# Two-layer hybrid encoder, one core: projections that fill TensorE's waits move from 64x64 tiles to the whole array in part, and items, weights and merges are reordered

## The reference, cut to what matters

```
x += 1/2 * g0 * norm(swiglu(mod0(norm(x))))
x +=       g1 * norm(mixer(mod1(norm(x))))      # h = mod1(norm(x))
x += 1/2 * g2 * norm(swiglu(mod2(norm(x))))

proj = h @ w_in                                  # columns for r, m, d and the gates
y_r = rwkv7(...)      # 16 heads x 64, delta rule in both directions
y_m = mamba2(...)     # z (2048 columns), xbc (3072, depthwise conv over 5 tokens, then silu), dt
y_d = diff_attention  # q, k, v (3072 columns), 8 heads, two softmax maps per head
merged = g[0]*(y_r @ w_br_r) + g[1]*(y_m @ w_br_m) + g[2]*(y_d @ w_br_d)
mixer = merged @ w_out
```

## Time and profile before

| | |
|---|---|
| median of 3 runs | 2737.28 us (2736.98 to 2739.47) |
| the profiled execution's own time | 2737.22 us |
| its span, first to last instruction | 2735.5 us |
| instructions of the program | 66483 |
| busy: PE / DVE / ACT / POOL | 2620.0 / 1413.6 / 499.4 / 232.0 us |
| mean granted TensorE clock | 0.993 of 2.4 GHz |
| moved by DMA | 445.12 MB |

### The profile page before, as it was taken

The page is one execution under the profiler, slowest core; times in us unless marked ns, Lnnn a source line. Parts: engine busy times, 40 slices in busy tenths (PEclk is TensorE's granted clock), DMA queues, the critical chain, the costliest instruction groups (busy, mean ns, idle before and its releaser), DMA issues.

```text
span 2735.5 us, 66483 instructions
## 1 busy us (share of the span) xinstructions
PE 2620.0 (96%) x30077; PEld 1906.3 (70%) x30077; DVE 1413.6 (52%) x2560; ACT 499.4 (18%) x1016; POOL 232.0 (8%) x372
## 2 busy tenths in 40 slices
PE   6999999999999999999999999999999899999999
PEld 6777877777775555577787778777778745546776
DVE  3552465677775856312035425456787768562001
ACT  1000223122222332100010011322222223221000
POOL 6000102000001101100000010110000011100000
PEclk9999999999999999999999999999999999999999
DMA  9894433322327542484469734423222275424452
GB/s 364 309 337 151 133 117 123 111 83 92 116 80 239 169 168 94 144 291 165 157 242 340 271 128 142 152 91 113 87 83 88 91 253 191 143 96 154 138 168 93
DMA packets 226348, 445.12 MB, mean 163 GB/s; under 512 B 7545, under 2 KB 102327, under 8 KB 226065
## 3 DMA queue, kind: packets, MB, share of 16 engines
q1 hardware_dynamic: 211376, 395.59, 41.5%
q0 software_dynamic: 12960, 38.98, 4.5%
q10 hardware_dynamic: 1728, 6.29, 0.6%
HBM read 422.88 MB, written 17.96 MB: 161 GB/s over the span
## 4 chain that ended last, share of the span: by engine, by line
PE 81%; DVE 11%; ACT 3%; issue 2%; DMA 2%; POOL 1%; DVEq 0%; ACTq 0%; SPq 0%; POOLq 0%
PE ps L1039 79%; DVE scratch L2228 5%; DVE scratch L2231 2%; DVE scratch L2234 1%; DVE gbc L2234 1%; PE ps L1068 1%; DVE scratch L2544 1%; DMA scratch<-in_ada_w 1%; DMA ring<-in_w_in 1%; DMA scratch<-acs_scratch 0%; DMA acs_scratch<-scratch 0%; ACT scratch L2053 0%; ACT scratch L2051 0%; ACT scratch L2200 0%; DVE x L2234 0%
## 5 line engine op out<-in xcount | busy, mean ns | idle before, releaser
L1039 PE MATMUL ps<-hT,ring 64*64 64x256 f32 (+3 forms) x9472 | 1147.9, 367 | 8.3 <-issue 3.1
L1039 PEld LDWEIGHTS ps<-hT,ring 64*64 64x64 f32 (+2 forms) x9472 | 943.0, 160 | 155.9 <-issue 35.8
L1039 PE MATMUL ps<-scratch 64*64 64x32 f32 (+6 forms) x15264 | 846.7, 255 | 56.8 <-DVE scratch L2228 16.1
L1039 PEld LDWEIGHTS ps<-scratch 64*64 64x64 f32 (+2 forms) x15264 | 592.6, 140 | 332.3 <-issue 206.2
L2228 DVE TENSOR_TENSOR scratch<-scratch,ps 128x256 f32<-128x256 f32 (+3 forms) x314 | 155.2, 494 | 661.1 <-ACT scratch L1895 533.1
L1039 PE MATMUL ps<-ring,hT 64*64 64x256 f32 (+2 forms) x2816 | 425.4, 421 | 5.3 <-DVE scratch L2234 2.6
L1039 PEld LDWEIGHTS ps<-ring,hT 64*64 64x64 f32 (+1 forms) x2816 | 228.7, 149 | 143.3 <-issue 116.8
L2228 DVE TENSOR_TENSOR scratch<-scratch 128x512 f32<-128x512 f32 (+4 forms) x426 | 276.1, 648 | 75.4 <-ACTq L2035 31.8
L1039 PE MATMUL ps<-ring,scratch 128*128 128x512 f32 x512 | 234.7, 593 | 0.5
L2234 DVE SCALAR_TENSOR_TENSOR scratch<-scratch,ccol 128x1024 f32<-128x1024 f32 x120 | 154.2, 1285 | 15.2 <-DMA scratch<-in_ada_w 11.3
L1895 ACT ACTIVATE scratch<-ps 128x512 f32<-128x512 f32 x40 | 23.9, 597 | 746.1 <-PE ps L1039 746.1
(11 more groups left out here) (228 smaller groups left out, 1392.8 us busy)
## 6 DMA issues: line engine op xcount, KB each, us to landing
ring<-in_w_in SPq DMA_DIRECT2D x56, 2048.0 KB, 9.0
ring<-in_ffn_w SPq DMA_DIRECT2D x88, 1024.0 KB, 9.0
scratch<-in_ada_w SPq DMA_DIRECT2D x35, 2048.0 KB, 16.2
scratch<-in_ffn_w SPq DMA_DIRECT2D x44, 1024.0 KB, 5.0
ring<-in_w_branch_mamba SPq DMA_DIRECT2D x8, 2048.0 KB, 8.0
scratch<-acs_scratch POOLq DMA_DIRECT2D x24, 512.0 KB, 5.8
scratch<-fill_scratch SPq DMA_DIRECT2D x16, 512.0 KB, 8.7
ring<-in_w_branch_rwkv SPq DMA_DIRECT2D x4, 2048.0 KB, 11.1
```

Source lines behind the costliest of these rows:

```text
L1039: return pe.matmul(o, lhsT, rhs, start=start, stop=stop)
```

## The change

- `FILL` gets a new order (c 0 comes before z 3, and so on). The steps are distributed anew over pairs and places, still 448 from pair 0 on; the levels lose steps in pairs 1 to 3 (3 to 2 in each), the place `s2` gains (4 to 6 in most pairs), and `fill(p, "k4")` is new, in the last level.
- `fill_mixed` replaces `fill_tiles`: steps at the places `TILE_POINTS` (`r0` to `u3`) are on tiles, a multiple of four of them in an item, and all others on the whole array. By the table, 112 of the 448 steps of a layer are on tiles and 336 on the whole array. Six items of 14 have no tile step and so no wait between turns.
- ACT's `conv_sigmoid` is put ahead of the item copies at `k4` and `u0`. The first convolution moves from pair 2 to pair 1, with three taps in a level.
- POOL computes `group_norm_rstd` before `next_pair`, and stores z 3 one pair later.
- The FFN's second weights are issued on ACT's queue instead of SP's.
- In attention, `beside` gets one more product before the last transposes of a head; the merges of the Mamba branch are cut in halves and put into heads 2, 3, 5 and 6; the attention branch's products are reordered so that 21 of 32 can come before the last rows of the last head, and its merges are reordered. The first output weights are loaded in two parts, the first earlier.
- At the start of layer 0, ACT instead of DVE copies the parameters (line 2343).

```diff
-FILL = [("z", 0), ("z", 1), ("z", 2), ("z", 3), ("c", 0), ("q", 0), ("c", 1), ("q", 1), ("c", 2), ("q", 2),
-        ("c", 3), ("q", 3), ("c", 4), ("c", 5), ("v", 0), ("v", 1)]
+FILL = [("z", 0), ("z", 1), ("z", 2), ("c", 0), ("z", 3), ("c", 1), ("q", 0), ("c", 2), ("q", 1), ("c", 3),
+        ("q", 2), ("c", 4), ("q", 3), ("c", 5), ("v", 0), ("v", 1)]
 # columns: ops mid lv k0 k1 k2 k3 (k4) r0 u0 s1 r1 u1 s2 r2 u2 s3 r3 u3 end
-FILL_PAIR = ((8, 8, 8, 2, 2, 2, 2, 0, 2, 0, 1, 1, 4, 1, 2, 0, 2, 2, 3),
-             (14, 10, 10, 3, 3, 3, 3, 0, 2, 0, 1, 1, 4, 1, 2, 0, 2, 2, 3),
-             (14, 10, 10, 3, 3, 3, 3, 0, 2, 0, 1, 1, 4, 1, 2, 0, 2, 2, 3),
-             (14, 10, 10, 3, 3, 3, 3, 0, 2, 0, 1, 1, 4, 1, 2, 0, 2, 2, 3),
-             (14, 8, 7, 1, 2, 2, 2, 0, 1, 0, 1, 1, 3, 1, 1, 0, 1, 1, 3),
-             (11, 8, 8, 2, 2, 2, 2, 0, 2, 0, 1, 2, 4, 2, 2, 0, 2, 2, 9),
-             (8, 8, 8, 2, 2, 2, 2, 0, 2, 0, 1, 1, 4, 1, 2, 0, 2, 2, 3),
-             (14, 8, 7, 1, 2, 2, 2, 0, 1, 0, 1, 1, 3, 1, 1, 0, 1, 1, 0))
+FILL_PAIR = ((7, 8, 8, 2, 2, 2, 2, 1, 0, 1, 0, 1, 1, 4, 1, 1, 0, 1, 1, 2),
+             (12, 7, 7, 2, 2, 2, 2, 1, 0, 2, 0, 1, 1, 6, 1, 2, 0, 1, 2, 2),
+             (13, 8, 7, 2, 2, 2, 2, 1, 0, 2, 0, 1, 2, 6, 1, 2, 0, 2, 2, 2),
+             (13, 8, 7, 2, 2, 2, 2, 1, 0, 2, 0, 1, 1, 6, 1, 2, 0, 2, 2, 2),
+             (13, 9, 9, 2, 3, 3, 3, 3, 0, 2, 0, 1, 1, 6, 1, 2, 0, 2, 2, 2),
+             (13, 8, 9, 3, 3, 3, 3, 3, 0, 1, 0, 1, 1, 4, 1, 1, 0, 1, 1, 2),
+             (12, 7, 7, 2, 2, 2, 2, 1, 0, 2, 0, 1, 1, 6, 1, 2, 0, 1, 2, 2),
+             (13, 8, 7, 2, 2, 2, 2, 1, 0, 2, 0, 1, 1, 6, 1, 2, 0, 2, 2, 8))
+TILE_POINTS = ("r0", "u0", "s1", "r1", "u1", "s2", "r2", "u2", "s3", "r3", "u3")
-CONV_AT_LEVELS = CONV_SIGMOID = {2: 0, 3: 1, 4: 2, 5: 3, 6: 4, 7: 5}
+CONV_AT_LEVELS = CONV_SIGMOID = {1: 0, 3: 1, 4: 2, 5: 3, 6: 4, 7: 5}
@@ PE
+                def fill_mixed(i):
+                    on_tiles = tile_steps(i)
+                    split = sum(on_tiles) // 4
+                    tiles = [(turn, h, k) for turn in range(2) for k in range(split) for h in range(2)]
+                    whole = [(r, h, k) for k in range(split, KT) for r in range(2) for h in range(2)]
+                    order = [tiles.pop(0) if on else whole.pop(0) for on in on_tiles]
...
+                        if on and (x, h, k) == (1, 0, 0):
                             pe.wait_ge(*fill_done(l, 2 * i + 1))
...
-                        if k < LV - 1:
-                            fill(p, f"k{k}")
+                        fill(p, f"k{k}")
...
+                    first = [(0, k, t) for k in range(late) for t in range(TT)] + [(1, k, 0) for k in range(late)]
+                    behind = [(0, late, 0), (0, late, 1), (1, late, 0)] + [(1, k, 1) for k in range(KT)]
...
-                    beside(3 if h == 0 else 2)
+                    beside(4 if last else 3 if h == 0 else 2)
...
-                    beside(4 if h == 0 else 3)
+                    beside(3 if last else 4)
@@ ACT
+                down_weights(0)
+                down_weights(1)
                 for j in range(FJ - 1):
...
+                    if j:
+                        act.wait_ge(*down_done(l, f * FJ + j))
+                        down_weights(j + 1)
...
+            act.wait_ge(*params_turned(0, 1))
+            act.activation(prm[:, :], ps[:, 3, :], ACT.Identity).then_inc(params_evac.sem, 1)
...
                     if q:
+                        fill_evacuations(q - 1, "lv")
                         fill_evacuations(q - 1, "k3")
                         if q - 1 in CONV_SIGMOID:
                             conv_sigmoid(CONV_SIGMOID[q - 1])
+                        fill_evacuations(q - 1, "k4")
                         fill_evacuations(q - 1, "u0")
@@ DVE
                         if p in CONV_AT_LEVELS:
-                            convolve(2 if d else 4)
+                            convolve((4 if d else 0) if p == 1 else (2 if d else 4))
...
                         if k < LV - 1 and p in CONV_AT_LEVELS:
-                            convolve(2)
+                            convolve(3 if p == 1 else 2)
...
+                    if h in (2, 3):
+                        mamba_gated(0, h - 2)
+                    if h == 6:
+                        mamba_gated(1, 1)
...
+                    if h in (2, 3):
+                        mamba_added(0, h - 2)
+                    if h == 5:
+                        mamba_gated(1, 0)
+                    if h == 6:
+                        mamba_added(1, 1)
...
-                merge(IT_BM, 1, 2, sg_second, (1,))
-                merge(IT_BD, 2, 1, sg_first, (0,))
```

More of the change, by code:

```diff
@@ L105, with tile_steps @@
 assert filled(PAIRS - 1, "end") == UNITS * UNIT_STEPS
+def tile_steps(i):
+    on_tiles = [False] * sum(c for _, c in FILL_EARLY)
+    for row in FILL_PAIR:
+        for point, c in zip(FILL_POINTS, row):
+            on_tiles += [point in TILE_POINTS] * c
+    steps = on_tiles[2 * UNIT_STEPS * i:2 * UNIT_STEPS * (i + 1)]
+    kept = sum(steps) // 4 * 4
+    return [on and sum(steps[:n]) < kept for n, on in enumerate(steps)]
 COND = 9
@@ L161, in loads_before @@
 def loads_before(item, parity):
-    return sum(2 if n in FFN_ITEMS else 1 for n in range(item) if n % 2 == parity)
-CONV_AT_LEVELS = CONV_SIGMOID = {2: 0, 3: 1, 4: 2, 5: 3, 6: 4, 7: 5}
+    return sum(2 if n in FFN_ITEMS or n == IT_OUT else 1 for n in range(item) if n % 2 == parity)
+CONV_AT_LEVELS = CONV_SIGMOID = {1: 0, 3: 1, 4: 2, 5: 3, 6: 4, 7: 5}
 C_CONVW, C_V0 = 0, 120
@@ L1328, in fill_tiles @@
                     pe.wait_ge(*fill_evac(l, 2 * i))
[L1329 to L1330 removed]
+                    for n, (on, (x, h, k)) in enumerate(zip(on_tiles, order)):
+                        if on and (x, h, k) == (1, 0, 0):
                             pe.wait_ge(*fill_done(l, 2 * i + 1))
[L1332 to L1335, removed]
[L1336 to L1344 removed]
@@ new lines, in fill_mixed @@
+                        for r in range(2) if on else (x,):
+                            first, last = r not in begun, not any(o or y == r for o, (y, _, _) in zip(on_tiles[n + 1:], order[n + 1:]))
+                            begun.add(r)
+                            part = (r + x) % 2
+                            rows = slice(64 * part, 64 * part + 64) if on else slice(0, P)
+                            for cols in (slice(0, 64), slice(64, P)) if on else (slice(0, P),):
+                                w, m = fill_operands(i, r, h, k, rows, cols)
+                                ins = mm(ps[cols, FILL_BANKS[r], h * S:(h + 1) * S], w, m, first, last)
@@ L1346, in fill_products @@
+                        if n == 2 * UNIT_STEPS - 1 or (on and (x, h, k) == (0, 1, split - 1)) or (split == 0 and n == 0):
+                            ins.then_inc(fill_done.sem, 1)
+                        yield
                 def fill_products():
@@ L1709, in difference_products @@
                 def difference_products():
[L1711 removed]
+                    late = KT - 1
+                    first = [(0, k, t) for k in range(late) for t in range(TT)] + [(1, k, 0) for k in range(late)]
+                    behind = [(0, late, 0), (0, late, 1), (1, late, 0)] + [(1, k, 1) for k in range(KT)]
+                    for h, k, t in first + behind:
                         item = IT_BD + h
                         g, par = group_of(item), item % 2
[L1714 to L1729 removed]
@@ new lines, in difference_products @@
+                        if (k, t) == (0, 0):
+                            pe.wait_ge(*slot_loaded[par](l, loads_before(item, par) + 1))
+                            bank_free(l, g)
+                        if h == 0 and t == 0:
+                            pe.wait_ge(*yd_ready(l, k + 1))
+                        if (h, k, t) == (1, KT // 2, 1):
+                            pe.wait_ge(*hT_ready(l, 3))
+                            turn_tile(0, merged).then_inc(merged_turned.sem, 1)
+                        ins = mm(ps[:, 2 * (g % 2) + t, :], ydT[:, k, t * P:(t + 1) * P], slot(par)[:, k, :],
+                                 k == 0, k == KT - 1)
@@ L1991, in item_evacuate @@
                     act.wait_ge(*fill_evac(l, 2 * i + 2))
+                    if between is not None:
+                        conv_sigmoid(between)
                     if kind == "z":
```

153 lines of the change are left out of this document (75 added, 78 removed).

## The result

The changed kernel takes **2750.7 us** (median of 4 executions, 2747.5 to 2751.2) against 2737.2 before (4, 2737.0 to 2739.5): a ratio of 1.0044 with a 95% interval of 1.0031 to 1.0057. It is slower by more than the 0.2% that the prediction set as its bound. The forecast was 2725 in a range of 2703 to 2741: wrong in sign, and outside the range.

A forecast was written before the change was run, and what follows sets the result against it. The prediction took PE as the bound, busy 2620.0 of 2735.5 us. Inverse stages -1.8, attention -7 and the start -3 summed to -11.8 us, giving 2725 us in a range of 2703 to 2741.

The forecast's parts named there:

- "at nothing" for POOL's order: POOL's reordering in the inverse stage was put at no cost, its results being wanted later than it makes them.
- k4, -2.9: Last level of each pair: a whole step with its switch covers some 0.5 us of waiting for DVE; -2.9 us.
- pair 1, +0.8 for taps: Pair 1's levels: three taps bring DVE's cycle to about 3.5 us against PE's 3.4; +0.8 us.
- the number of places: Inverse stages: 6 new whole fillings in each of 16 pairs, 96 switches at 0.32 us, +30.7 us.
- the switch in the levels: A whole filling put into tile work costs 0.20 to 0.48 us, taken as 0.32.
- The slow rival: A switch costs a whole latency each way, about 0.6 us a filling, giving 2752 us; chance 0.17.
- the issue waits: Inverse stages: with 2016 records less in either, half of PE's 18.8 us of issue waits goes; -9 us.
- line 1979's sigmoid ahead of u0: Pairs 2, 3 and 6, both layers: ACT's sigmoid ahead of the copies ends DVE's 2.20 us wait; -10 us.
- s2 (pair 1): At s2, pairs 0 to 6, added steps fill PE's 1.1 us lost to DVE's scan; -7.5 us.
- Attention's -7: Attention: filled transpose waits and cut merges, less new waits, give -3.5 us a layer, -7 us in all.
- The start, -3,: Start of layer 0: with the parameter copy on ACT, DVE's conditioning sum goes as its data land; -3 us.

The follow-up runs named there:

- e14: Changed kernel with POOL's product of z3 moved ahead of the norm's power and pair 3's loads: 2750.0 us, ratio 1.0040.
- e13: Changed kernel with the steps at k0 to k4 of pairs 1 and 7 alone put on tiles: 2738.4 us, ratio 0.9997.
- e12: Changed kernel with POOL's product of z3 with its sigmoid cut to 64 of 1024 columns, output incomplete: 2743.9 us, ratio 1.0024.
- e6: e4 with the steps at k0 to k4 on tiles too: 2714.3 us, ratio 0.9922.
- e5: Changed kernel with all steps of items 2 to 15 on tiles and the first convolution item back in pair 2: 2713.9 us, ratio 0.9923.
- e3: Kernel before with the mixed filling alone, its old distribution of steps and order of items kept: 2756.9 us, ratio 1.0069.
- e7: Kernel before with the attention part of the change alone: 2728.9 us, ratio 0.9975.
- e10: The changed kernel run once more, unchanged: 2749.9 us, ratio 1.0050.
- e4: Changed kernel with the first convolution item back in pair 2, z3 ahead of c0: 2729.9 us, ratio 0.9978.
- e1: Changed kernel with all steps of items 2 to 15 on tiles: 2724.7 us, ratio 0.9956.
- e9: e4 with mid, lv and k0 to k4 on tiles too, whole steps at ops and end alone: 2710.4 us, ratio 0.9910.
- e2: Kernel before with the attention part, the start and the w2 loads on ACT's queue alone: 2724.7 us, ratio 0.9957.

## Why the prediction was wrong, by its own steps

**The step that failed** is one that the sum does not have. Every duration was taken at the clock of the kernel before, 0.99 in the inverse stage, and I asked of each new wait how long it is, never what the clock does behind it. Mean clock before: 0.993. After: 0.988. On 2745 us that is 0.005 x 2745 = 14 us. From the forecast 2725 to 2751 it is 25 us, so the clock is the larger half of the miss and the next steps are the rest. The inverse stages whole, before and then after:

```profile
420.19:836.90 416.71, 388.79 (x10369) 318.99 (x10368) 295.52 (x672) 94.31 (x176) 36.66 (x49) 0.99 0.29 97
1764.37:2186.08 421.71, 389.95 (x10369) 319.91 (x10368) 295.47 (x672) 94.32 (x176) 36.44 (x49) 0.99 0.28 96
```

```profile
420.42:861.98 441.56, 419.12 (x8353) 339.40 (x8351) 299.74 (x679) 93.88 (x175) 37.12 (x50) 0.95 0.27 91
1780.64:2206.01 425.37, 403.13 (x8353) 325.11 (x8351) 299.79 (x679) 93.90 (x175) 37.12 (x50) 1.00 0.28 94
```

In time times clock, which takes out what the lower level cost, before and after are both at about 2718 (2737.2 x 0.993 and 2750.7 x 0.988): apart from the clock the rearrangement moves nothing that this can see. That is a conversion, not a measurement, and a clock given to three digits leaves 1.4 us open on either side. The measurements are e14, whose executions at 0.994 are as fast as the kernel before, and e13, with 12 us back and the clock at 0.992, some 10 of them the clock's.

**Second: "at nothing" for POOL's order.** I asked only whether its results come in time. Its product of z3 now meets DVE's products at the opening of pair 2: 2.49 us of waiting in layer 0 and 2.13 in layer 1, and behind each wait 3.4 us at the lower clock, which cost about 1.7 more and belong to the first step. e12, without them, is 6.8 us faster.

**Third: k4, -2.9.** F, k4 and E of the last level take 2.63 us (1.05, 0.63, 0.95, from start to start) where F and E took 2.07: the step of 0.44 costs 0.56, so +0.12 x 16 = +2. The wait that it was to cover is still there, behind it. That E of the other levels does not wait for DVE had no row, and I mistook the chain step's wait for E4's.

**Fourth: pair 1, +0.8 for taps.** The four taps of `mid` and three of the level stand in DVE's queue ahead of what E0 and F1 want: 0.69 and 1.20 us of idle time, then 0.35 in every level, in layer 1, where the clock stayed up. The level takes 3.59 us there (1854.38 to 1857.97) where the forecast had 3.5. By my estimate that is about 2 us a layer more than forecast, and in layer 0 the two waits are what stood just ahead of the fall.

**Fifth: the number of places.** The forecast priced 96, and k4's 16 apart. There are 132: it missed the 20 in the recurrence where a step is left over.

**Right:** the switch in the levels, forecast at 0.32: 0.32 by the timeline and 0.30 by time (e6). Over all places it is lower, 0.22 (e5) and, from e3, (18.6 + 8.2) / 126 = 0.21, so that the sum of the switches, 132 x 0.22 = 29, comes out near the 35.8 that the forecast had with k4's; the places missed and the price that was too high outside the levels cancel in part, which is luck. The slow rival had the right total and the wrong mechanism: it asked for 0.6.

Also right: the issue waits, half gone (18.9 to 9.8, -9.1 of -9). For those the Trainium skill, "Runtime: NRT & Kernel Launch", Instruction fetch mechanics, calls the cost of fetching mostly hidden, by which nothing was to be had; these waits came down by 9 us with 8067 instructions less. That they are fetching at all no row says, and the halving was a guess between two bounds that came true. DVE has no wait for line 1979's sigmoid ahead of u0. At s2 (pair 1) the records of six steps take 3.02 us where the pace gives 2.62, the turn included. Attention's -7 came by time in e7.

**The start, -3,** gave less. The first product of the FFN comes 3.0 us earlier (34.5 for 37.5), behind a wait of 2.7 us for `in_ffn_w`. Of the lead 1.3 us are left at the end of the FFN (275.6 for 276.9). Those are lost at 385, where the clock is at its lower level for 6.8 us and not 3.4: the inverse stage begins at 420.4, for 420.2 before.

```profile
PE ps L1041 <- DMA ring<-in_ffn_w: 3.4, 2, 2.7
```

**Not seen at all:** behind the product of `prow` PE waited 3.18 us for DVE in the kernel before and does not now, in both layers: the last convolution item ends earlier in the new order. That is about -6.4, and two falls of the clock of 3.4 us that stood behind these waits (from 843.7 and 2191.9) went with them.

```profile
842.17 0.68 PE L1039 MATMUL ps<-stack_i,scratch 64*64 64x64 f32 x16 [3.18 <-DVE scratch L2228]
```

```profile
864.00 0.68 PE L1041 MATMUL ps<-stack_i,scratch 64*64 64x64 f32 x16
```

**The account** of the profiled span, 22 us above the forecast's -12: clock in the inverse stages 13.7 (stretches at half rate of 44.4 us in all there, 17.0 before, half of each lost), the waits of pair 2 4.6, k4 5, pair 1 about 3, the start's gain lost 3, less the 6.4 at `prow` and some 5 more in the rest of the layers, 3.4 of which are those two falls of the clock. This leaves about 4, and the 20 places that the forecast did not count come to 3 at 0.15 each. These are estimates from the traces of two executions. The median stands 3.2 above the profiled execution.

**Open:** what decides whether the clock falls at a given wait. Layer 0 and layer 1 have the same two waits and one of them falls; e10 has both, and e12 and e14, with the same two waits up to there, have it in layer 0 and not at all. No run here separates the length of the wait from the work around it.

## What to carry to other kernels

Put a change of filling where another kind of work stands anyway, and price the others by two levels laid side by side; 0.3 us is small until there are 132. Count the places from the table of steps, left-over ones too. Judge each new wait on a TensorE program twice: for its length, and for what the granted clock does behind it, and compare time and clock together before an edit is blamed. When an engine's queue is reordered, look at what the others run at that moment, not only at who wants its results; and ask of every added place which item it lets end there.

## What the runs showed of the hardware

- A fall of the granted clock begins at the same point with either filling, but lasted 13.7 us with whole-array steps between the levels and 3.4 with tiles (e4, e6); in pair 1 of layer 0 it was 23.9 and 3.4 (the changed kernel, e1).
- The same program spreads over 27 us, and its mean clock with it: 2735.0 at 0.994, 2762.6 at 0.982 (e14).
- A DVE product with both inputs in SBUF took 3.18 us beside POOL's product of 2.35, and 0.42 elsewhere; even an operation of four columns took 1.86 in place of 0.17 (e14).
- With the new arrangement TensorE's issue waits rose with the number of instructions: 9.8 to 11.9 us at 58416, 13.5 at 58800 (e13), 16.3 at 60144 (e6), 19.8 at 63408 (e9), 24.8 to 26.9 at 66480 (e5, e1). The number is not all: the kernel before, e7 and e2 have 18.5 to 18.9 at about 66490.
